# A two-block transformer kernel on one Trainium2 core: rows of the activations' buffer 516 columns apart, and two buffers in the other order

## The chip, the core and the metric

The kernel runs on one core of a Trainium2 chip (trn2) as one launch. The metric is the device time of an execution in microseconds; several runs are made and their median is taken. PE is TensorE, DVE is VectorE, ACT is ScalarE, POOL is GpSimd, SP the engine that issues most DMAs. SBUF is the on-chip memory of 128 partitions; an address in it is a byte offset that is the same in every partition.

## The reference

256 tokens of 1024 features go through two blocks, each of two layers. The first block has a convolution layer and an attention layer, each followed by an MLP; the second has a gated mixer layer and a windowed attention layer with a context of 256 further tokens. Cut to the products of weights and activations, which take nearly all of the work:

```python
def first_block(x, ...):
    for i in range(2):
        h = rms_norm(x, mix_norm_g[i]) * (1.0 + sc1) + sh1
        y = conformer_conv(h, ...) if i == 0 else moba_attention(h, ...)   # 1024 -> 2048, -> 1024; 1024 -> 3072, -> 1024
        x = x + g1 * y
        h = rms_norm(x, mlp_norm_g[i]) * (1.0 + sc2) + sh2
        x = x + g2 * (jnp.square(jax.nn.relu(h @ mlp_w1[i])) @ mlp_w2[i])  # 1024 -> 4096 -> 1024
    return x

def second_block(x, ...):
    for i in range(2):
        h, hc = x * (1.0 + scale) + shift, ctx * (1.0 + scale_c) + shift_c
        out = mixer_a(h, ...) if i == 0 else mixer_b(h, hc, ...)           # 1024 -> 6144, 2048 -> 1024; 1024 -> 2560, -> 1024
        x = layer_norm_2(alpha * x + gate * out, ln_g[i], ln_b[i])
    return x
```

All values are float32. `sh1`, `sc1` and the like are modulation vectors, products of a conditioning vector with a weight matrix.

## The kernel before

The weights are cut into units of 1024 × 256 (`UNITS`), which stream from HBM into four places of `raw` in the order of their use. Activations are kept with features on partitions: a tensor of 1024 features and 256 tokens is 8 tiles (index `k`) of 128 partitions × 256 columns.

A product is made in split precision. An fp32 operand is written as `hi + lo`, both of type float32r, and three products are summed in PSUM: `hi·hi`, `hi·lo`, `lo·hi`. ScalarE writes `w_hi` (L641) and VectorE `w_lo` (L1083) for each unit of weights, two units ahead. The split activations lie in two buffers:

- `X_both`, shape [128, 2, 8, 512]: the input of most units. Index 1 is hi or lo (`XH`, `XL`), index 2 the tile `k`, and of a row's 512 columns the first 256 are the tokens, the others the context's tokens in the second block. One more use: at one place the split weights of a unit are put into columns 256 to 511.
- `F_both`, shape [128, 2, 4096]: the inner activations of the MLPs and of the mixer, and at three places split weights (`AHEAD`). Within a half the rows follow each other at 256 or 512 columns.

PE runs a unit in one of two forms. `three` makes three matmuls for each tile `k` and each half `i` of the unit's columns. `joined`, used by the units of the list `JOINED`, makes two: the first reads hi and lo of the activations as one moving operand of 2 pieces × 256 columns, one half of the buffer's whole length apart.

```python
def three(out, lhs_hi, lhs_lo, rhs_hi, rhs_lo, start, stop):
    mm(out, lhs_hi, rhs_hi, start=start, stop=False)                          # L1894
    mm(out, lhs_hi, rhs_lo, start=False, stop=False)                          # L1895
    return mm(out, lhs_lo, rhs_hi, start=False, stop=stop)                    # L1896
...
def joined(out, lhs_hi, lhs_lo, rhs, start, stop):
    mm(out.rearrange("p (h t) -> p h t", h=2), lhs_hi, rhs, ...)              # L1900, rhs = both[:, :, k, 0:T]
    return mm(out[:, 0:T], lhs_lo, rhs[:, 0, :], ...)                         # L1901
```

For the units that make values (`v`, `b_v`, `a_v`) the activations are the stationary operand, in slices of 128 tokens, and the weights move. Between the products stand boundaries, where a norm is taken and ScalarE and VectorE fill `X_both` tile by tile (`biased_hi` L671, `scale_and_split` L1320 and their like), attention, and the convolution (L1879: plain float32 matmuls, four at a time, over shifted copies of a buffer; a step's start is 4 columns behind the last's).

Buffers are allocated one behind the other in the order in which `sb(...)` names them, and instructions stand in each engine's queue in the order of the code, with semaphores between engines. Before the change `X_both` begins at byte 83072 of a partition and `F_both` at 115840, then follow `V` at 148608, `HT`, `cond`, `dot`, `EV`, `WS`, `BS`, `SM` and the small ones.

Of the kernel before, what the change touches and what calls it, by code (L numbers as in the profile page):

```python
# [28 lines left out]
P = 128  # L29
D = 1024  # L30
KT = D // P
T = 256
# [21 lines left out]
F32R = mybir.dt.float32r  # L54
# [223 lines left out]
def build(nc, stream, first_in, cols_in, cond_in, const_in, x_in, ctx_in, ws_in, bs_in, out):  # L278
    with ExitStack() as ctx:
        def sb(name, shape, dt=F32):  # L280
            return ctx.enter_context(nc.sbuf_tensor(name, shape, dt))
# [6 lines left out]
        w_lo = sb("w_lo", [P, SPLITS, KT, UC], F32R)  # L288
        X = sb("X", [P, KT, T])
        C = sb("C", [P, KT, T])  # L290
        X_both = sb("X_both", [P, 2, KT, 2 * T], F32R)
        F_both = sb("F_both", [P, 2, 2 * KT * T], F32R)
        V = sb("V", [P, 8192])
        HT = sb("HT", [P, KT * T])
        cond = sb("cond", [P, 2, D])
# [63 lines left out]

        U = V[:, 0:KT * (T + PAD)].rearrange("p (k t) -> p k t", k=KT)  # L360
        CV = V[:, 2304:2304 + 2048].rearrange("p (k t) -> p k t", k=KT)
        TS = V[:, 4352:4352 + 2048].rearrange("p (k t) -> p k t", k=KT)

        Q = V[:, 0:2048].rearrange("p (k t) -> p k t", k=KT)
        K1 = V[:, 2048:4096].rearrange("p (k t) -> p k t", k=KT)
        V1 = V[:, 4096:6144].rearrange("p (t c) -> p t c", t=2)

# [2027 lines left out]
```

How the kernel before makes its waits and increments, by code:

```python
        @block.sync  # L577
# [4 lines left out]
            sp.dma_start(col[:, 0:early_cols], cols_in[:, 0:early_cols]).then_inc(params_loaded, 16)  # L582
            sp.dma_start(X[:, :, :], x_in).then_inc(x_loaded, 16)
            for i in range(len(FIRST_CHUNKS)):
                for n in (2 * i, 2 * i + 1):
                    sp.dma_start(first_at[n], first_in[n]).then_inc(first_loaded[n], 16)
                if i in (1, 3, 5):
                    n = i // 2
                    sp.dma_start(raw[:, n, :], stream[n]).then_inc(slot_loaded[n], 16)
            sp.dma_start(col[:, early_cols:], cols_in[:, early_cols:]).then_inc(late_loaded, 16)
            sp.dma_start(con[:, early_con:], const_in[:, early_con:RESIDENT]).then_inc(late_loaded, 16)
            sp.wait_ge(first_dotted, 1)
            for n in range(FIRST_UNITS, NS):
                if EARLY <= n < EARLY + 2:
                    sp.wait_ge(first_dotted, n)
                elif EARLY + 2 <= n < EARLY + 2 + FIRST_UNITS:
                    sp.wait_ge(unit_done, n - EARLY - 1)
                elif n == EARLY + 2 + FIRST_UNITS:
                    sp.wait_ge(unit_consumed, consumed(FIRST_UNITS))
                elif n > EARLY + 2 + FIRST_UNITS:
                    sp.wait_ge(unit_consumed, consumed(n - RING))
                sp.dma_start(places[PLACE[n]], stream[n]).then_inc(slot_loaded[PLACE[n]], 16)
                if n == WHERE[MLP0 + 20]:
                    sp.wait_ge(acts_lo, SET[2])
```

## Time and profile before

| | |
|---|---|
| median of 3 runs | 1204.58 us (1203.28, 1204.62, 1204.58) |
| span of the profiled execution | 1199.6 us; its own time is not listed apart from the three, and 5.0 us lie between the median and the span |
| PE busy | 1173.5 us, 98%, 7486 matmuls |
| DVE, ACT, POOL busy | 910.5 us (76%), 598.2 us (50%), 58.9 us (5%) |
| DMA | 229.48 MB, 191 GB/s over the span |

A matmul's busy time runs from its start until its last result is written, so neighbours overlap, and the pace of PE is to be read from the starts in the timeline. A group of the profile gives line, engine, operation, output and inputs by buffer, the count, and the mean time of one; `X_both,w_hi` as inputs means that both were read, the moving one named first where the shapes say nothing else.

### The profile page before, as it was taken

The page shows a single profiled execution, that of the slowest core. Times are in us where ns is not written, and L with a number is a line of the kernel's source. Part 1 is how long each engine was busy: PE and PEld are TensorE (multiplying, and loading weights), DVE is VectorE, ACT ScalarE, POOL GpSimd, SP SyncE. Part 2 cuts the span into 40 slices and gives each one's busy share as a digit, 9 for nine tenths or more (in the row PEclk, how much of TensorE's full clock was granted, in tenths as well). Part 3 has the DMA queues.
Part 4 walks back from the last instruction along what each step waited for, and adds up shares of the span by engine and source line. Part 5 has one row for each costly group of instructions (what it writes and reads, how often), then busy time and mean ns, then how long its engine had stood idle before and what let it go on. Part 6 is the DMA issues. An engine that isn't in the chain of part 4 may idle for free.

```text
span 1199.6 us, 18278 instructions
## 1 busy us (share of the span) xinstructions
PE 1173.5 (98%) x7486; PEld 1006.4 (84%) x7486; DVE 910.5 (76%) x1372; ACT 598.2 (50%) x800; POOL 58.9 (5%) x85
## 2 busy tenths in 40 slices
PE   8998999999999999999999999999999999999997
PEld 6876988888988868899999888888888888898776
DVE  6798788888888677999977664885856676677757
ACT  4597666546544365865465333232212333454873
POOL 0110000000000040000000000000000000000640
PEclk9999999999999999999999999999999999999998
DMA  9994578787768604777765353342444342343000
GB/s 371 333 340 173 211 282 293 281 313 278 278 241 307 225 21 161 266 261 253 275 238 181 141 194 122 140 150 97 152 164 141 110 155 93 125 141 106 2 1 36
DMA packets 34470, 229.48 MB, mean 191 GB/s; under 512 B 4033, under 2 KB 4801, under 8 KB 8146
## 3 DMA queue, kind: packets, MB, share of 16 engines
q1 hardware_dynamic: 33874, 227.14, 52.1%
q0 software_dynamic: 512, 1.16, 0.4%
q8 instruction: 59, 0.97, 0.3%
q14 instruction: 25, 0.20, 0.0%
HBM read 226.08 MB, written 1.05 MB: 189 GB/s over the span
## 4 chain that ended last, share of the span: by engine, by line
PE 83%; DVE 7%; ACT 5%; issue 2%; DMA 2%; SPq 1%; POOL 1%; ACTq 0%; DVEq 0%
PE prod L1900 17%; PE prod L1894 16%; PE prod L1895 15%; PE prod L1896 15%; PE prod L1901 9%; ACT w_hi L641 2%; DMA WS<-first_chunks 2%; DVE w_lo L1083 1%; PE misc L2056 1%; PE misc L2158 1%; PE misc L1809 1%; PE prod L2146 1%; PE misc L1853 1%; PE prod L2133 1%; DVE raw L1116 1%
## 5 line engine op out<-in xcount | busy, mean ns | idle before, releaser
L1083 DVE TENSOR_TENSOR w_lo<-raw,w_hi 128x2048 fp32r<-128x2048 f32 x129 | 295.4, 2290 | 196.4 <-ACT w_hi L641 196.1
L641 ACT ACTIVATE w_hi<-raw 128x2048 fp32r<-128x2048 f32 x129 | 247.1, 1915 | 379.0 <-PE prod L1896 229.0
L1894 PE MATMUL prod<-X_both,w_hi 128*128 128x256 f32 (+1 forms) x656 | 217.7, 332 | 1.6 <-DVE X_both L1320 1.3
L1895 PE MATMUL prod<-X_both,w_hi 128*128 128x256 f32 (+1 forms) x656 | 214.4, 327 | 0.0
L1896 PE MATMUL prod<-X_both,w_lo 128*128 128x256 f32 (+1 forms) x656 | 214.4, 327 | 0.0
L1900 PE MATMUL prod<-X_both,w_hi 128*128 128x512 f32 x592 | 211.3, 401 | 1.8 <-DVE X_both L1320 1.8
L1901 PE MATMUL prod<-X_both,w_lo 128*128 128x256 f32 x592 | 165.8, 280 | 0.0
L1900 PEld LDWEIGHTS prod<-X_both,w_hi 128*128 128x128 f32 x592 | 111.1, 188 | 32.1 <-DVE X_both L1320 3.0
L1894 PEld LDWEIGHTS prod<-X_both,w_hi 128*128 128x128 f32 x656 | 124.5, 190 | 15.6 <-DVE X_both L1320 1.9
L1895 PEld LDWEIGHTS prod<-X_both,w_hi 128*128 128x128 f32 x656 | 124.5, 190 | 10.8 <-issue 0.5
L1896 PEld LDWEIGHTS prod<-X_both,w_lo 128*128 128x128 f32 x656 | 124.5, 190 | 10.7
L1894 PE MATMUL prod<-F_both,w_hi 128*128 128x256 f32 (+1 forms) x384 | 122.8, 320 | 0.2 <-DVE w_lo L1083 0.2
L1896 PE MATMUL prod<-F_both,w_lo 128*128 128x256 f32 (+1 forms) x384 | 122.3, 318 | 0.0
L1895 PE MATMUL prod<-F_both,w_hi 128*128 128x256 f32 (+1 forms) x384 | 122.3, 318 | 0.0
L1901 PEld LDWEIGHTS prod<-X_both,w_lo 128*128 128x128 f32 x592 | 111.7, 189 | 0.0
L1116 DVE CUSTOM_DVE_ANT_0 raw<-raw,cond 128x1024 f32<-128x1024 f32 x80 | 94.0, 1216 | 0.0
L1900 PE MATMUL prod<-F_both,w_hi 128*128 128x512 f32 x256 | 90.5, 398 | 0.0
L1894 PEld LDWEIGHTS prod<-F_both,w_hi 128*128 128x128 f32 x384 | 72.9, 190 | 5.8 <-DVE w_lo L1083 0.6
L1896 PEld LDWEIGHTS prod<-F_both,w_lo 128*128 128x128 f32 x384 | 72.9, 190 | 5.0
L1895 PEld LDWEIGHTS prod<-F_both,w_hi 128*128 128x128 f32 x384 | 72.9, 190 | 4.9
L1901 PE MATMUL prod<-F_both,w_lo 128*128 128x256 f32 x256 | 71.9, 281 | 0.0
L1894 PE MATMUL prod<-w_hi,X_both 128*128 128x256 f32 (+1 forms) x192 | 66.0, 344 | 0.0
(331 smaller groups left out, 1959.5 us busy)
## 6 DMA issues: line engine op xcount, KB each, us to landing
raw<-stream SPq DMA_DIRECT2D x200, 1024.0 KB, 4.9
V<-first_chunks SPq DMA_DIRECT2D x8, 512.0 KB, 12.0
V<-stream SPq DMA_DIRECT2D x2, 1024.0 KB, 17.4
X<-x_features SPq DMA_DIRECT2D x1, 1024.0 KB, 5.2
raw<-first_chunks SPq DMA_DIRECT2D x2, 512.0 KB, 6.4
C<-first_chunks SPq DMA_DIRECT2D x2, 512.0 KB, 17.1
V<-cond_rows SPq DMA_DIRECT2D x1, 1024.0 KB
C<-ctx_features SPq DMA_DIRECT2D x1, 1024.0 KB, 7.1
```

The lines of the kernel that those rows point to most:

```text
L641: A(halves(w)[0], places[PLACE[n]].rearrange("p (k c) -> p k c", k=KT), ACT.Copy).then_inc(weight_hi, 1)
L1083: ins = tt(lo, places[PLACE[n]].rearrange("p (k c) -> p k c", k=KT), hi.bitcast(F32), ALU.subtract)
L1116: ins = vec.tensor_tensor_reduce(w, w, cond[:, 0, :], 1.0, 0.0, ALU.mult, ALU.add, got[:, 0, k:k + 1])
L1809: ins = mm(misc[:, bank, c:c + T], ones, src[:, k, :], start=(k == 0), stop=(k == count - 1), skip_group_check=True)
L1853: ins = mm(misc[:, b, 0:1], H[:, k, P * b:P * (b + 1)], ones[:, 0:1], start=(k == 0), stop=(k == KT - 1), skip_group_check=True)
L1894: mm(out, lhs_hi, rhs_hi, start=start, stop=False)
L1895: mm(out, lhs_hi, rhs_lo, start=False, stop=False)
L1896: return mm(out, lhs_lo, rhs_hi, start=False, stop=stop)
L1900: mm(out.rearrange("p (h t) -> p h t", h=2), lhs_hi, rhs, start=start, stop=stop)
L1901: return mm(out[:, 0:T], lhs_lo, rhs[:, 0, :], start=False, stop=stop, skip_group_check=True)
L2056: ins = mm(misc[:, i, P * t:P * (t + 1)], VA[:, t, c:c + P], WS[:, j, :], start=True, stop=True)
L2133: ins = mm(score_pair(p)[:, 512 * off:512 * (off + 1)], q, key, start=(term == 0), stop=(term == 2))
```

## The change

The two allocations are written in the other order, and a row of `X_both` becomes 516 columns, of which the last 4 are never used. The code that indexes the buffers is the same, and so are the instructions and their order on every engine.

```diff
@@ build
         X = sb("X", [P, KT, T])
         C = sb("C", [P, KT, T])
-        X_both = sb("X_both", [P, 2, KT, 2 * T], F32R)
         F_both = sb("F_both", [P, 2, 2 * KT * T], F32R)
+        X_both = sb("X_both", [P, 2, KT, 2 * T + 4], F32R)
         V = sb("V", [P, 8192])
```

| bytes in a partition | before | after |
|---|---|---|
| start of `F_both` | 115840 | 83072 |
| start of `X_both` | 83072 | 115840 |
| from a row `k` of `X_both` to the next | 2048 | 2064 |
| from hi to lo in `X_both` | 16384 | 16512 |
| from hi to lo in `F_both` | 16384 | 16384 |
| start of `V` (all behind it moves alike) | 148608 | 148864 |

## Rows read from the trace of the kernel before

**Rows 1.** The page: busy us, share of the span, instructions; PE's granted clock by slices.

```profile
PE 1173.5 (98%) x7486; PEld 1006.4 (84%) x7486; DVE 910.5 (76%) x1372; ACT 598.2 (50%) x800; POOL 58.9 (5%) x85
...
PEclk9999999999999999999999999999999999999998
```

**Rows 2.** The page: the chain that ended last, by engine and by line.

```profile
PE 83%; DVE 7%; ACT 5%; issue 2%; DMA 2%; SPq 1%; POOL 1%; ACTq 0%; DVEq 0%
PE prod L1900 17%; PE prod L1894 16%; PE prod L1895 15%; PE prod L1896 15%; PE prod L1901 9%; ACT w_hi L641 2%; DMA WS<-first_chunks 2%; DVE w_lo L1083 1%; PE misc L2056 1%; PE misc L2158 1%; PE misc L1809 1%; PE prod L2146 1%; PE misc L1853 1%; PE prod L2133 1%; DVE raw L1116 1%
```

**Rows 3.** Lines L1894 and L1900, reads of X_both: count, ns min/median/max, first and last start.

```profile
L1894 PE MATMUL prod<-X_both,w_hi x656: 278/283/681, 45.0 to 1187.6; 128*128 128x256 f32 x96, 128*128 128x512 f32 x68
L1894 PE MATMUL prod<-w_hi,X_both x192: 277/389/792, 388.3 to 1112.4; 128*128 128x256 f32 x96, 128*128 128x512 f32 x96
L1894 PE MATMUL misc<-w_hi,X_both x32: 389/389/389, 685.1 to 744.3; 128*128 128x512 f32 x32
L1894 PE MATMUL prod<-X_both x16: 280/283/467, 1039.3 to 1044.9; 128*128 128x256 f32 x16
...
L1900 PE MATMUL prod<-X_both,w_hi x592: 391/398/504, 145.3 to 1178.7; 128*128 128x512 f32 x198
L1900 PE MATMUL prod<-X_both,F_both x48: 392/395/403, 151.5 to 484.9; 128*128 128x512 f32 x48
```

**Rows 4.** Timeline of PE from 250 us: start us, us, engine line op.

```profile
249.72 0.40 PE L1900 MATMUL prod<-F_both,w_hi 128*128 128x512 f32 x1
249.96 0.28 PE L1901 MATMUL prod<-F_both,w_lo 128*128 128x256 f32 x1
...
250.78 0.40 PE L1900 MATMUL prod<-F_both,w_hi 128*128 128x512 f32 x1
```

**Rows 5.** Timeline of PE from 600 us.

```profile
599.89 0.39 PE L1900 MATMUL prod<-X_both,w_hi 128*128 128x512 f32 x1
600.12 0.28 PE L1901 MATMUL prod<-X_both,w_lo 128*128 128x256 f32 x1
...
600.93 0.39 PE L1900 MATMUL prod<-X_both,w_hi 128*128 128x512 f32 x1
```

**Rows 6.** Stretches, line L1900 alone: us, PE busy (x), PEld, PEclk, DMA, GB/s.

```profile
151.50:298.40 146.90, 146.90 (x417) 78.07 (x417) 1.00 0.80 291
479.75:507.40 27.65, 27.65 (x81) 14.85 (x80) 1.00 0.72 267
...
598.50:609.60 11.10, 11.10 (x32) 5.86 (x32) 1.00 0.72 247
```

**Rows 7.** Timeline of PE from 639.8 us and from 800 us.

```profile
639.73 0.28 PE L1895 MATMUL prod<-F_both,w_hi 128*128 128x256 f32 x1
...
641.17 0.28 PE L1895 MATMUL prod<-F_both,w_hi 128*128 128x256 f32 x1
...
800.25 0.39 PE L1894 MATMUL prod<-X_both,w_hi 128*128 128x512 f32 x1
...
801.38 0.39 PE L1896 MATMUL prod<-X_both,w_lo 128*128 128x512 f32 x1
```

**Rows 8.** Timeline of PE at 90 us; lines L2146, L1609, L1360 and L1305 as rows 3.

```profile
89.78 0.39 PE L1879 MATMUL prod<-V,HT 128*32 128x256 f32 x3
...
91.08 0.39 PE L1879 MATMUL prod<-V,HT 128*32 128x256 f32 x3
...
L2146 PE MATMUL prod<-con,C x64: 272/273/331, 1114.1 to 1159.4; 128*128 128x128 f32 x64
...
L1609 DVE TENSOR_SCALAR C<-C,sm x16: 485/488/490, 1111.5 to 1156.4; 128x512 f32<-128x512 f32 x16
...
L1360 DVE SCALAR_TENSOR_TENSOR V<-prod,col,EV x8: 474/476/485, 44.0 to 86.3; 128x256 f32<-128x256 f32 x8
...
L1305 DVE SCALAR_TENSOR_TENSOR HT<-X,mod,misc x24: 471/474/482, 143.6 to 477.3; 128x256 f32<-128x256 f32 x24
```

## Prediction

> **What bounds the kernel now.** I read the busy shares first. TensorE (PE) is busy 1173.5 us of a span of 1199.6 us, 98%, VectorE 76%, and PE's granted clock stands at its upper level in 39 of the 40 slices [rows 1]. The chain of work that ended last gives the same answer: 83% of it is PE, and its five largest entries are the five lines that multiply split operands, L1894 to L1896 (`three`) and L1900, L1901 (`joined`), 17 + 16 + 15 + 15 + 9 = 72% of the span [rows 2]. So time is made of how far apart these matmuls start. Everything that the change could do to VectorE, ScalarE or a DMA has 26 us of PE idleness as its only way in.
>
> The busy time of a matmul in the groups is its whole passage (398 ns for 512 columns) and overlaps the next; the distance from start to start is what counts, and the timeline has it. Four rhythms matter:
>
> - `joined` pairs (512 columns in two pieces, 256 of `hi` and 256 of `lo`, then 256 columns): in one stretch three pairs take 250.78 − 249.72 = 1.06 us, 353.3 ns a pair [rows 4]. In another three pairs take 600.93 − 599.89 = 1.04 us, 346.7 ns [rows 5]. Both repeat to the nanosecond over whole units; I call them the slow and the quick rhythm. From 151.5 to 298.4 us 416 pairs run (417 less the one cut at the edge) in 146.9 us, 353.1 ns each; from 479.8 to 507.4 us 80 pairs in 27.65 us and from 598.5 to 609.6 us 32 pairs in 11.1 us, 345.6 and 346.9 ns each [rows 6]. I went through all 56 blocks of 16 pairs in the timeline, of which these stretches hold 33: 42 are slow, 11 quick, and 3 are among waits.
> - `three`, 256 columns: 12 starts from 639.73 to 641.17 us, 120.0 ns each. `three`, 512 columns in one piece: 5 starts from 800.25 to 801.38 us, 226 ns each [rows 7].
>
> A quick pair costs what its parts cost, 120 + 226 = 346 ns. A slow one costs 353.3 − 346.7 = 6.7 ns more.
>
> **The change, part by part.** Nothing is removed, added or moved on any engine: every queue holds the same instructions in the same order with the same waits. Only addresses differ. `X_both` rows go from 512 to 516 columns, 2048 to 2064 bytes; its `hi` and `lo` halves from 16384 to 16512 bytes apart; `F_both` takes the old place of `X_both` with its shape unchanged; what is allocated behind (`V`, `HT`, `cond`, `EV`, `WS` and the rest) lies 256 bytes further on. The terms:
>
> 1. *PE reads `X_both` as the moving operand*: 3 × (656 + 16) + 2 × (592 + 48) = 3296 matmuls; *as the stationary operand*: 3 × (192 + 32) = 672 [rows 3]. Together 3968, half of them on an odd k, where a row now starts 16 bytes off any larger power of two. Does the place of a row matter to PE? The trace has three tests. First, the slow rhythm repeats every 3 pairs while k repeats every 8 and the column half every 16: the row's number has no part in it. Second, `F_both` (rows of 1024 bytes) and `X_both` (rows of 2048) show the same 353.3 and 346.7 ns. Third, where operands do start off large powers of two: the convolution reads its shifted rows from a start that moves by 16 bytes with each step of four matmuls, and six such steps take 91.08 − 89.78 = 1.30 us, 216.7 ns each, equal all along; the transposes of the scores read rows 513 columns apart (2052 bytes) and take 272 to 273 ns at the median and minimum in both buffers [rows 8]. These are plain fp32 matmuls, which stream at half the columns per time of the fp32r ones, so the test isn't complete. Taken at 0; bounds below.
> 2. *ScalarE and VectorE write and read `X_both`* in rows of 256 columns at each boundary. Starts off large powers of two leave VectorE as it is: scaling a row of the 513-column buffer takes 485 to 490 ns for starts at 0, 4 and 8 bytes alike; the write into `V` behind 31 columns of padding takes 474 to 485 ns, the write at an even start 471 to 482 ns [rows 8]. At most 5 ns × the 8 tiles of a boundary × 9 boundaries = 0.4 us. Taken at 0.
> 3. *The buffers behind, 256 bytes further on*: their starts keep every divisor up to 256. No row tests more; taken at 0.
> 4. *`F_both` and `X_both` trade places*: both already stood at two different places and gave one rhythm. 0.
>
> Sum: 0 us on a span of 1199.6 us. Around the span lie 1204.58 − 1199.6 = 5.0 us of the median run (the three runs lie from 1.3 below to 0.04 above it). The profiled execution's own time isn't given apart from these, so the sum stands against 1199.6 + 5.0. I take 1204.3 us: the two rhythms can change from one execution to the next, there are 42 slow blocks against 11 quick ones, so a reshuffle has more room downward. One block is worth 16 × 6.7 = 107 ns.
>
> The bounds. Downward: the two-piece read is the only thing that differs between a pair and its parts, and its pieces lie 16384 bytes apart. If that distance makes the 6.7 ns, the slow blocks on `X_both` (28 of the 42, `F_both` having 14) turn quick: 28 × 0.107 = 3.0 us. If the new timing also tips the other 14, 42 × 0.107 = 4.5 us. Upward: if each read or load on an odd k costs one such step of 6.7 ns, 3968 / 2 × 6.7 = 13.3 us.
>
> Further down than that: a `three` matmul of 256 columns takes 120.0 ns, while a column at 2.4 GHz is 0.417 ns and 256 of them 106.7 ns; 13.3 ns go to something. All fp32r operands now start at equal distances from multiples of 512 bytes, so a collision that depends on bits below that couldn't be told from a fixed cost. If it were one and odd k escaped it, 1984 × 13.3 = 26 us would go. I give this 1 in 50: the 512 columns of a `three` (213.3 ns at 2.4 GHz) take 226 ns, so the excess is 13 ns there too, though loads and moving reads lie at other distances in time.
>
> On collisions the Trainium skill ("SBUF — State Buffer", section "SBUF: two separate sides") says that only the port pair of VectorE and GpSimd and the DMA side have contention, and that PE and ACT never wait on anyone. By it the padding can gain nothing and the time stays 1204.6 us; the trace agrees for the DMAs, since the slow pair keeps its 353.1 ns over 146.9 us in which they move 291 GB/s [rows 6]. The same page ("Door 1: The DMA port swizzle") speaks of lines of 16 bytes in SBUF with a penalty for each crossing. 2064 is 129 × 16, so by it a row crosses as many lines as before and the slower rival below falls away; no run here shows it for fp32r.
>
> **The rivals.**
>
> *A, nothing but noise* (forecast): 1204.3 us, its own range 1202.3 to 1206.0. It covers a reshuffle of the rhythms: all 11 quick blocks to slow is +1.2 us, a dozen slow ones to quick −1.3 us, about the spread of the three runs. 0.66.
>
> *B, the pieces 16384 bytes apart collide*: 1201.6 us if `X_both` alone heals, 1200.1 us if all does. For it: the excess sits in the two-piece matmul alone. From its start to the next matmul's it takes 249.96 − 249.72 = 0.24 us in the slow rhythm [rows 4] and 600.12 − 599.89 = 0.23 us in the quick one [rows 5]. Against it: the same 16384 bytes give 346.7 ns elsewhere, on both buffers, so the distance doesn't decide by itself; how a block is entered does. 0.16, with the 26 us case 0.02 more.
>
> *C, the other side: odd rows cost PE a step.* The mechanism is one extra fetch at the start of a row that lies 16 bytes off, in the L1894 to L1901 matmuls. Full price +13.3 us, 1217.9 us; if only the 640 two-piece reads pay, on odd k and at both pieces, 320 × 2 × 6.7 = 4.3 us, 1208.9 us. It decides (over 0.2%, 2.4 us) from 360 steps of 6.7 ns on. Against it the evenness of the convolution and of the 513-column rows. 0.12, and 0.04 for a slower shift that I can't name.
>
> **How the numbers follow.** A measurement of this kernel can tell about 0.2%, 2.4 us, from no change: below 1202.2 is faster, above 1207.0 slower. A gives 0.66 same. B's cases both lie below 1202.2: with the 26 us case 0.18 faster. C and the unnamed shift 0.16 slower. The range takes in A and both ends of B, down to 1199.8, and upward A and the edge of the same: 1207.0. Left out are C and the 26 us case.
>
> **What the changed kernel's profile would show.** If A: `joined` pairs at 353.3 or 346.7 ns and nothing between, 120 and 226 ns for `three`, on odd and even k alike; PE busy within 1 us of 1173.5 us plus or minus the count of slow blocks times 0.107 us. If B: 346.7 ns in all pairs on `X_both`, and still 353.3 ns in some on `F_both`. If C: a start-to-start distance that alternates with k on `X_both` and not on `F_both`. The groups of ScalarE and VectorE on `X_both` keep their means within 5 ns in each case. I'd be wrong if row starts below 512 bytes matter to fp32r reads at full rate, which no row of before can show.

## The result and the profile after

The changed kernel takes 1206.87 us (median of 20 runs, 1203.75 to 1209.19); the kernel before takes 1204.2 us in 20 runs (1202.31 to 1208.32). The ratio is 1.0017 with a 95% interval of 1.0010 to 1.0025: 1.2 to 3.0 us slower (2.0 by the ratio; the two medians differ by 2.7), small and real.

The page of the changed kernel, its busy times and the chain by line:

```profile
span 1204.2 us, 18278 instructions
...
PE 1179.6 (98%) x7486; PEld 1006.3 (84%) x7486; DVE 910.7 (76%) x1372; ACT 598.4 (50%) x800; POOL 58.9 (5%) x85
...
PE prod L1900 17%; PE prod L1894 15%; PE prod L1895 15%; PE prod L1896 15%; PE prod L1901 8%; ACT w_hi L641 2%; DMA WS<-first_chunks 2%; DVE w_lo L1083 1%; PE misc L2056 1%; PE misc L1809 1%; PE misc L2158 1%; PE prod L2146 1%; PE prod L2133 1%; DVE raw L1116 1%; PE prod L1861 1%
```

VectorE and ScalarE stand where they stood [rows 1]; PE is busy 6.1 us longer, but busy time doesn't tell the effect: two kernels below whose paces are those of before (`h1_order_look`, `i1_all_32`) had 1177.8 and 1178.5 us. This execution took 1205.98 us, 1.8 us more than its span, so the profiled one of before, with its 1199.6 us, took an estimated 1201.4 us, less than any of the 20 listed, and the two profiles exaggerate the difference.

The timeline of PE in the changed kernel, at both ends of five stretches of 24 matmuls within one unit (start us, us, engine, line):

```profile
180.87 0.40 PE L1900 MATMUL prod<-X_both,w_hi 128*128 128x512 f32 x1
...
185.05 0.39 PE L1900 MATMUL prod<-X_both,w_hi 128*128 128x512 f32 x1
...
622.04 0.28 PE L1894 MATMUL prod<-F_both,w_hi 128*128 128x256 f32 x1
...
624.92 0.28 PE L1894 MATMUL prod<-F_both,w_hi 128*128 128x256 f32 x1
...
704.28 0.40 PE L1894 MATMUL prod<-w_hi,X_both 128*128 128x512 f32 x1
...
709.88 0.40 PE L1894 MATMUL prod<-w_hi,X_both 128*128 128x512 f32 x1
...
912.57 0.39 PE L1894 MATMUL prod<-X_both,w_hi 128*128 128x512 f32 x1
...
918.14 0.39 PE L1894 MATMUL prod<-X_both,w_hi 128*128 128x512 f32 x1
...
1060.60 0.28 PE L1894 MATMUL prod<-X_both,w_hi 128*128 128x256 f32 x1
...
1063.42 0.28 PE L1894 MATMUL prod<-X_both,w_hi 128*128 128x256 f32 x1
```

Divide each stretch by its 24 matmuls. 512 columns moving from `X_both`: 5.57 us, 232 ns each, where rows 7 have 226. 512 columns of weights against a stationary slice of `X_both` (`w_hi,X_both`): 5.60 us, 233 ns. 256 columns from `X_both`: 2.82 us, 117.5 ns, where 120.0 stood on either buffer. 256 columns from `F_both`: 2.88 us, 120.0 ns as before [rows 7]. Pairs on `X_both`: 4.18 us for 12, 348.3 ns, neither of the rhythms of [rows 4, 5]. All that touches the padded buffer has a new pace, in both directions, and on `F_both` the `three` matmuls keep the old ones.

Means over all matmuls of a kind (from the starts in the timeline, those behind a wait left out), in ns:

| start to start | count | before | after | count × difference |
|---|---|---|---|---|
| 512 columns moving from `X_both` | 816 | 226.8 | 231.5 | +3.8 us |
| 512 columns of weights, `X_both` stationary | 384 | 226.8 | 232.7 | +2.3 us |
| 256 columns moving from `X_both` | 1152 | 119.8 | 117.6 | −2.6 us |
| 256 columns of weights, `X_both` stationary | 288 | 119.8 | 118.3 | −0.4 us |
| pairs on `X_both` (592 and 48) | 640 | 351.8 | 349.1 | −1.7 us |
| pairs on `F_both` | 256 | 352.6 | 349.2 | −0.9 us |
| 256 and 512 columns on `F_both` | 1152 | 120.0, 226.8 | 120.0, 226.9 | 0 |

They add up to +0.5 us, short of the measured 2.0. The two rows of pairs depend on how many of the 56 blocks happened to be slow in the one execution of before that was profiled: 44 with the 3 blocks among waits sorted in. Two experiments below with the same distances between operands had 28 and 41. With 28 instead of 44, before would be 1.7 us shorter in those rows, and the sum +2.2 us; with 41 it would be +0.8 us.

The two spans differ by more, 4.5 us. Matmul by matmul, the starts give +0.7 us in the steady stretches of the five lines, +0.9 us in the waits among them and +2.9 us in the matmuls outside of them. Much of the last two is PE's granted clock (the figure ahead of the last two; the first two lines are of before, the others of after):

```profile
325.00:335.00 10.00, 9.18 (x68) 8.36 (x68) 5.15 (x12) 2.95 (x9) 0.00 (x0) 1.00 0.56 211
465.00:475.00 10.00, 9.53 (x69) 8.46 (x67) 5.74 (x15) 3.62 (x10) 0.00 (x0) 1.00 0.56 211
...
325.00:335.00 10.00, 9.78 (x60) 8.70 (x58) 4.12 (x13) 3.01 (x8) 0.00 (x0) 0.83 0.55 211
465.00:475.00 10.00, 10.00 (x61) 8.99 (x60) 5.52 (x16) 4.09 (x10) 0.00 (x0) 0.83 0.57 210
```

The levels of the clock are 1.2 and 2.4 GHz, so 0.83 over 10 us is the lower one for an estimated third of the time. Ahead of the last 15 us, the execution before had such a fall in one place (near 110 us), the one after in four (near 100, 140, 330 and 470 us). From 135 to 152 us the changed kernel loses 1.5 us and from 300 to 345 us 1.0 us. The falls don't go with the padding: `h1_order_look` and `i1_all_32`, with the paces of before, had them in five and four places, and `f2_rows_only`, with the paces of after, in two. It keeps 1.00 from 325 to 335 us and loses nothing from 300 to 345 us.

ScalarE and VectorE write the padded rows at the old pace, to within 1 and 4 ns at the median (lines L671 and L1320 of the changed kernel; count, ns min/median/max):

```profile
L671 ACT ACTIVATE X_both<-HT,mod x24: 491/509/514, 144.9 to 477.0; 128x256 fp32r<-128x256 f32 x24
...
L1320 DVE SCALAR_TENSOR_TENSOR X_both<-HT,mod,X_both x24: 476/480/486, 145.5 to 477.5; 128x256 fp32r<-128x256 f32 x24
```

### The profile page after: what moved, and what is told of

It is laid out like the page before. It is cut to its first block, busy times and chain, and to the rows that moved or that the text cites. A ratio compares the mean times of both kernels' runs of the same rounds, so it can differ in the third digit from the quotient of the medians.

```text
span 1204.2 us, 18278 instructions
## 1 busy us (share of the span) xinstructions
PE 1179.6 (98%) x7486; PEld 1006.3 (84%) x7486; DVE 910.7 (76%) x1372; ACT 598.4 (50%) x800; POOL 58.9 (5%) x85
## 4 chain that ended last, share of the span: by engine, by line
PE 81%; DVE 8%; ACT 5%; issue 2%; DMA 2%; SPq 1%; POOL 1%; ACTq 0%; DVEq 0%
PE prod L1900 17%; PE prod L1894 15%; PE prod L1895 15%; PE prod L1896 15%; PE prod L1901 8%; ACT w_hi L641 2%; DMA WS<-first_chunks 2%; DVE w_lo L1083 1%; PE misc L2056 1%; PE misc L1809 1%; PE misc L2158 1%; PE prod L2146 1%; PE prod L2133 1%; DVE raw L1116 1%; PE prod L1861 1%
## 5 line engine op out<-in xcount | busy, mean ns | idle before, releaser
L1894 PE MATMUL prod<-X_both,w_hi 128*128 128x256 f32 (+1 forms) x656 | 217.8, 332 | 2.3 <-DVE X_both L1320 1.3
L1900 PE MATMUL prod<-X_both,w_hi 128*128 128x512 f32 x592 | 209.5, 397 | 0.2 <-DVE X_both L1320 0.2
L1894 PEld LDWEIGHTS prod<-X_both,w_hi 128*128 128x128 f32 x656 | 123.2, 188 | 18.3 <-DVE X_both L1320 1.9
L1900 PEld LDWEIGHTS prod<-X_both,w_hi 128*128 128x128 f32 x592 | 111.2, 188 | 28.5 <-DVE X_both L1320 0.8
L1894 PE MATMUL prod<-F_both,w_hi 128*128 128x256 f32 (+1 forms) x384 | 122.8, 320 | 0.2 <-DVE w_lo L1083 0.2
L1900 PE MATMUL prod<-F_both,w_hi 128*128 128x512 f32 x256 | 89.8, 396 | 0.0
L1894 PEld LDWEIGHTS prod<-F_both,w_hi 128*128 128x128 f32 x384 | 73.1, 190 | 6.0 <-DVE w_lo L1083 0.8
L1894 PE MATMUL prod<-w_hi,X_both 128*128 128x256 f32 (+1 forms) x192 | 66.4, 346 | 0.0
```

The lines of the kernel that those rows point to most:

```text
L1900: mm(out.rearrange("p (h t) -> p h t", h=2), lhs_hi, rhs, start=start, stop=stop)
```

## The experiments

"Distance" below is the start of the moving operand minus that of the stationary one, modulo 256 bytes. In the kernel before it is 0 for all large matmuls: `w_hi`, `w_lo`, `X_both` and `F_both` begin at 33920, 50304, 83072 and 115840, all 128 past a multiple of 256, and their rows and slices are multiples of 512 or 256 bytes long. Line numbers shift by 1 or 2 where the edit adds lines.

### The parts of the change, one at a time

**The order alone** (`f1_order_only`, `h1_order_look`)

```diff
-        X_both = sb("X_both", [P, 2, KT, 2 * T], F32R)
         F_both = sb("F_both", [P, 2, 2 * KT * T], F32R)
+        X_both = sb("X_both", [P, 2, KT, 2 * T], F32R)
```

> The two buffers in the other order, rows still 512 columns apart. Theory T1 (what counts is where a row of X_both starts within a small power of two): every start is again a multiple of 128 bytes, so the distances from start to start go back to those of before, 120.0 and 226.8 ns for three, and 346.7 or 353.3 ns for a joined pair; time within 1.2 us of before. Rival T2 (the place of the buffers or the 256 bytes by which the rest moves counts): 231.5 ns for 512 columns on X_both and +2 us as in the changed kernel. Rival T3 (only the share of slow and quick joined rhythms moved, by chance): 226.8 ns too, time anywhere within 2 us.

> The order alone again, for its profile (that of the run before was of a disturbed execution at half pace throughout; its other times were level with the kernel before). T1: 120.0 and 226.8 ns for three on both buffers, joined pairs at 346.7 or 353.3 ns. T2: 231.5 ns for 512 columns on X_both.

Ratio 1.0004 (0.9994 to 1.0014). `h1_order_look` is one more execution of the same kernel, 1203.31 us beside 1203.5, and its timeline shows:

```profile
910.49 0.39 PE L1894 MATMUL prod<-X_both,w_hi 128*128 128x512 f32 x1
...
915.93 0.39 PE L1894 MATMUL prod<-X_both,w_hi 128*128 128x512 f32 x1
```

24 matmuls in 5.44 us, 226.7 ns. Over all of them 226.8 and 119.8 ns, and 28 slow blocks, 26 quick. T2 falls: the order costs nothing. T1 holds, and T3 (chance alone) isn't told from it here.

**The rows alone** (`f2_rows_only`)

```diff
-        X_both = sb("X_both", [P, 2, KT, 2 * T], F32R)
+        X_both = sb("X_both", [P, 2, KT, 2 * T + 4], F32R)
         F_both = sb("F_both", [P, 2, 2 * KT * T], F32R)
```

> Rows 516 columns apart, the buffers in the old order (F_both and all behind it then start 256 bytes further on). T1: the changed kernel's distances on X_both return, near 231.5 ns for 512 columns, 117.6 ns for 256, 232.7 ns for 512 columns of weights against a stationary slice of X_both; F_both stays at 120.0 and 226.8 ns; +2 us (1 to 3). T2 (place or order): as before the change, 226.8 and 120.0 ns. T3: 226.8 and 120.0 ns, time within 2 us.

Ratio 1.0013 (1.0002 to 1.0024).

```profile
912.61 0.39 PE L1894 MATMUL prod<-X_both,w_hi 128*128 128x512 f32 x1
...
918.18 0.39 PE L1894 MATMUL prod<-X_both,w_hi 128*128 128x512 f32 x1
```

5.57 us, and over all: 231.5, 232.7 (weights moving) and 117.6 ns, the paces of the changed kernel to a tenth. `F_both`, which lies 256 bytes further on here, keeps 119.9 and 226.9 ns: a shift by 256 bytes is none. T1 holds so far; T2 and T3 fall.

### How far a start has to be off

**A constant shift** (`f3_base_16`)

```diff
+        gap_a = sb("gap_a", [P, 4])
         X_both = sb("X_both", [P, 2, KT, 2 * T], F32R)
+        gap_b = sb("gap_b", [P, 60])
         F_both = sb("F_both", [P, 2, 2 * KT * T], F32R)
```

> The old order and rows of 512 columns, but X_both starts 16 bytes further on (and 240 bytes are left behind it, so F_both and the rest move by 256). All rows then lie 16 bytes off a multiple of 64, alike for each k. T1 in the form 'a start off the boundary costs': 512 columns on X_both over 230 ns at every k with no alternation, +6 us or more than the changed kernel has from its 512-column matmuls, since there a quarter of the rows are on the boundary. T1 in the form 'what costs is that the offset changes from row to row': 226.8 and 120.0 ns at a constant offset, time as before. T5 (what counts is the offset between X_both and the weights read beside it): a new constant distance, either side of 226.8 ns.

The allocator rounds starts up to 32 bytes, so this kernel has both activation buffers at a distance of 32 bytes from the weights, alike for each k; it isn't the kernel that its expectation speaks of. Ratio 1.0026 (1.0016 to 1.0036).

```profile
911.67 0.40 PE L1896 MATMUL prod<-X_both,w_hi 128*128 128x512 f32 x1
...
917.27 0.40 PE L1896 MATMUL prod<-X_both,w_hi 128*128 128x512 f32 x1
...
1062.54 0.28 PE L1896 MATMUL prod<-X_both,w_hi 128*128 128x256 f32 x1
...
1065.34 0.28 PE L1896 MATMUL prod<-X_both,w_hi 128*128 128x256 f32 x1
```

512 columns: 5.60 us for 24, 233.3 ns, 6.6 more than at distance 0. 256 columns: 2.80 us, 116.7 ns, 3.3 less. All joined blocks are quick, 346.7 ns, but for the three whose weights lie in `F_both` and so moved along (distance 0, 353.3 ns). A steady offset has its own steady pace: what matters is not that the offset changes from row to row. It is what T5 said. Against the profiled execution before, the 512-column matmuls lose 10.3 us and all others win 10.0, so their paces alone give +0.3 us (+1.8 against `h1_order_look`); the measured 3.1 us (1.9 to 4.3) is more, and the rest isn't accounted for.

**Rows of 520 and of 528 columns** (`f4_rows_520`, `h4_rows_528`): the changed kernel with `2 * T + 8` and `2 * T + 16`; in the second `bst` lies in `GX` for room.

> As the changed kernel with rows of 520 columns: starts at 0 and 32 bytes within 64, by turns of two. T1 with a boundary of 64 bytes: distances off 226.8 and 120.0 ns again, repeating every 2 tiles k. T1 with a boundary of 32 bytes: all rows on it, 226.8 and 120.0 ns, time as before. T2 and T3 as in the run with the order alone.

> The changed kernel with rows of 528 columns (2112 bytes), so that each row starts on a multiple of 64 again; the small buffer bst lies in GX to make room. With a boundary of 64 bytes: 120.0 and 226.8 ns, joined pairs at 346.7 or 353.3 ns, time of before within 1.2 us. With a boundary of 128 bytes: 512 columns at 230 to 233 ns, repeating every 2 tiles k, +2 to +4 us.

Ratios 1.0032 (1.0019 to 1.0046) and 1.0026 (1.0017 to 1.0036). With 520 columns the 512-column matmuls on `X_both` take 232.4 ns, those of 256 columns 118.3 ns. With 528, where each row starts on a multiple of 64 and every second one 64 off a multiple of 128:

```profile
913.75 0.39 PE L1894 MATMUL prod<-X_both,w_hi 128*128 128x512 f32 x1
...
919.31 0.39 PE L1894 MATMUL prod<-X_both,w_hi 128*128 128x512 f32 x1
```

5.56 us, 231.7 ns. Boundaries of 32 and of 64 bytes both fall; being on a multiple of 64 isn't enough.

**16 bytes, by slicing** (`h2_start_16`)

```diff
-        X_both = sb("X_both", [P, 2, KT, 2 * T], F32R)
+        X_room = sb("X_both", [P, 2 * KT * 2 * T + 16], F32R)
...
+        X_both = X_room[:, 4:4 + 2 * KT * 2 * T].rearrange("p (h k t) -> p h k t", h=2, k=KT)
```

> Rows of X_both 512 columns apart, all of them shifted by 16 bytes by slicing from a larger buffer; F_both stays on multiples of 64. (In the run called f3_base_16 the allocator rounded each start up to 32 bytes, so there X_both, F_both and all behind them lay 32 bytes off a multiple of 64; it gave 233.3 ns for 512 columns and 116.7 to 117.3 ns for 256 on both buffers, and quick joined pairs throughout.) T6, what counts is the distance modulo 64 bytes between the moving operand's start and the stationary one's: a constant distance between 226.8 and 233.3 ns for 512 columns on X_both and between 116.7 and 120.0 for 256, with F_both at 120.0 and 226.8. T7, only 32 bytes count and 16 do not: 226.8 and 120.0 ns.

Ratio 1.0013 (0.9999 to 1.0026).

```profile
619.75 0.28 PE L1895 MATMUL prod<-F_both,w_hi 128*128 128x256 f32 x1
...
622.47 0.28 PE L1895 MATMUL prod<-F_both,w_hi 128*128 128x256 f32 x1
...
909.22 0.39 PE L1895 MATMUL prod<-X_both,w_hi 128*128 128x512 f32 x1
...
914.78 0.39 PE L1895 MATMUL prod<-X_both,w_hi 128*128 128x512 f32 x1
```

`X_both`: 231.7 ns for 512 columns, 113.3, 116.7 or 118.7 for 256 by unit, 346.7 or 360.0 a pair. T7 falls; T6 had the 512 columns right, but 113.3 ns lies below its 116.7. `F_both` didn't stay where it was, as I had meant: the 64 bytes of slack put it at distance 64, and there 24 matmuls of 256 columns take 2.72 us, 113.3 ns (117.8 in other units), 512 columns 228.9, and the pairs 353.3.

### Which operand's start counts

**The weights moved instead** (`h3_weights_32`): room between the two slots of `w_hi` and `w_lo`, and

```diff
+            c = (UNIT + 16) * (w % SPLITS) + (0 if UNITS[w][0] in WIDE else 8)
-            return w_hi[:, w % SPLITS], w_lo[:, w % SPLITS]
+            return [m[:, c:c + UNIT].rearrange("p (k c) -> p k c", k=KT) for m in (w_hi, w_lo)]
```

> Activations as before; the split weights of each unit whose matmuls move 256 columns or joined pairs start 32 bytes off a multiple of 64, those of units that move 512 columns stay on it. T6 (the distance between the two operands' starts counts): 256 columns at 117 ns instead of 119.8 (2208 matmuls, 6 us), joined pairs at 346.7 ns throughout (some 850 pairs at 5 ns, 4.5 us), 512 columns unchanged at 226.8; about 10 us faster, 1194 us. T8 (the moving operand's own start counts, the stationary one's doesn't): 119.8 ns and both joined rhythms, no change but for the value units, whose weights move: 1204 us.

Ratio 1.0048 (1.0035 to 1.0061), the slowest of all and far from my 1194. I had the sign of the distance wrong (moving minus stationary is −32 here, not +32), the second slots lay another 64 bytes off, and `w_lo` had moved by 128. The last makes one clean reading: a wide unit in the first slot has `w_hi` at distance 0 and `w_lo` at 128, the activations where they were.

```profile
913.26 0.39 PE L1896 MATMUL prod<-X_both,w_hi 128*128 128x512 f32 x1
...
918.81 0.39 PE L1896 MATMUL prod<-X_both,w_hi 128*128 128x512 f32 x1
```

5.55 us, 231.3 ns instead of 226.7. So the stationary operand's start counts (T8 falls), and 128 bytes count where 256 did not.

**Everything by 32 bytes** (`i1_all_32`): `in_front = sb("in_front", [P, 8])` ahead of `raw`.

> A spare tensor of 8 columns in front of everything: the weights, X_both, F_both and all the rest start 32 bytes further on, with all distances between them as before. T6 (only the distance between the moving and the stationary operand's start counts, modulo 256 bytes): 120.0 and 226.8 ns, joined pairs at 346.7 or 353.3, time of before within 1.2 us. T9 (each operand's own start within 256 bytes counts too): 512 columns above 230 ns or 256 columns below 118 ns, and the time off by 2 us or more to either side.

```profile
910.60 0.39 PE L1895 MATMUL prod<-X_both,w_hi 128*128 128x512 f32 x1
...
916.04 0.39 PE L1895 MATMUL prod<-X_both,w_hi 128*128 128x512 f32 x1
...
1057.49 0.28 PE L1895 MATMUL prod<-X_both,w_hi 128*128 128x256 f32 x1
...
1060.37 0.28 PE L1895 MATMUL prod<-X_both,w_hi 128*128 128x256 f32 x1
```

226.7 and 120.0 ns, 41 slow blocks and 13 quick, ratio 0.9992 (0.9978 to 1.0005). For a shift by 32 bytes it is the distance between the operands that counts and not where each lies. T9 falls for this shift.

**Distance +32 made by the weights** (`i2_weights_back_32`), and **+16 for some** (`i3_weights_back_16`): as `h3_weights_32` with slots 2112 columns apart, so that both arrays keep their place modulo 256, and 56 (or 60) for the 8.

> Activations as before; the split weights of the units that move 256 columns or joined pairs start 224 bytes past a multiple of 256 from where they did, so the moving operand's start minus the stationary one's is +32 modulo 256, as in the run f3_base_16; weights of units that move 512 columns keep distance 0 (bst lies in GX to make room). T6: 256 columns at 116.7 ns, joined pairs at 346.7 ns, 512 columns at 226.8; three-256 saves some 6 us, joined 4.5 us, so about 1194 us. T9: other distances, 256 columns anywhere from 113 to 119 ns and pairs up to 351 ns as in h3_weights_32.

> As i2_weights_back_32, but 240 bytes (moving minus stationary +16) for the units that make three matmuls of 256 columns, and 224 for joined pairs. T6: 113.3 or 116.7 ns for 256 columns, as X_both had in h2_start_16, 346.7 ns for a pair, 226.8 for 512; 1190 to 1193 us. T9: nothing can be said beforehand beyond 113 to 119 ns.

```profile
179.91 0.39 PE L1902 MATMUL prod<-X_both,w_hi 128*128 128x512 f32 x1
...
184.06 0.39 PE L1902 MATMUL prod<-X_both,w_hi 128*128 128x512 f32 x1
...
617.67 0.28 PE L1896 MATMUL prod<-F_both,w_hi 128*128 128x256 f32 x1
...
620.47 0.28 PE L1896 MATMUL prod<-F_both,w_hi 128*128 128x256 f32 x1
```

The same unit on `F_both` in `i3_weights_back_16`:

```profile
621.46 0.28 PE L1896 MATMUL prod<-F_both,w_hi 128*128 128x256 f32 x1
...
624.34 0.28 PE L1896 MATMUL prod<-F_both,w_hi 128*128 128x256 f32 x1
```

In `i2_weights_back_32` 12 pairs take 4.15 us, 346 ns each, and 256 columns 116.7 ns, as forecast; 512 columns stay at 226.8. 1195.48 us, ratio 0.9926 (0.9908 to 0.9945). The second missed: 256 columns at "distance 16" take 120.0 ns (2.88 us for 24), some 117.3, not the 113.3 to 118.7 that `X_both` showed when it was the one to move; 1198.08 us, ratio 0.9941 (0.9922 to 0.9961). At 16 bytes the distance alone doesn't give the pace, so T6 fails as a general rule and holds for the distances of 0 and +32 that were made in two ways.

### A version that beats both

**Activations of narrow units 32 bytes further right** (`i4_views_32`). Rows stay 512 columns apart and no buffer in front of `F_both` moves. The parts that only 256-column and joined matmuls read are written and read 8 columns further on; operands of 512 columns keep distance 0.

```diff
+        XHn, XLn = X_both[:, 0, :, 8:], X_both[:, 1, :, 8:]
-        F_hi = FH[:, :].rearrange("p (b k t) -> p b k t", b=2, k=KT)
+        F_hi = F_both[:, 0, 8:8 + 2 * KT * T].rearrange("p (b k t) -> p b k t", b=2, k=KT)
...
                         hi, lo, both = XH, XL, X_both
+                        if w < MIX_A or w >= B_OUT:
+                            hi, lo, both = XHn, XLn, X_both[:, :, :, 8:]
```

> Rows of 512 columns and all buffers where they were; the activations of units that move 256 columns (all of the first block and the last unit set) are put 8 columns further right in their rows of X_both, those of the MLPs 8 columns further in F_both (whose halves are 64 columns longer), while the operands of 512 columns keep their place. Both T6 and T9 say what f3_base_16 showed for these operands: 256 columns at 116.7 ns, joined pairs at 346.7, and 226.8 for 512 columns; 33 units of 48 matmuls at 3 ns less, 56 blocks of pairs at 5.5 ns less a pair: 9 us off, 1195 us. If only chance moved the rhythms: 1204 us.

```profile
179.98 0.39 PE L1901 MATMUL prod<-X_both,w_hi 128*128 128x512 f32 x1
...
184.14 0.39 PE L1901 MATMUL prod<-X_both,w_hi 128*128 128x512 f32 x1
...
618.62 0.28 PE L1895 MATMUL prod<-F_both,w_hi 128*128 128x256 f32 x1
...
621.42 0.28 PE L1895 MATMUL prod<-F_both,w_hi 128*128 128x256 f32 x1
...
903.63 0.39 PE L1895 MATMUL prod<-X_both,w_hi 128*128 128x512 f32 x1
...
909.07 0.39 PE L1895 MATMUL prod<-X_both,w_hi 128*128 128x512 f32 x1
```

346.7 ns a pair and no slow block, 116.7 and 226.7 ns. 1195.46 us, ratio 0.9927 (0.9907 to 0.9947): 8.8 us faster than before where 9 were forecast. In the profiled executions the starts of the large matmuls, waits included, add up to 955.6 us before and 948.1 us here, 7.5 less; their steady stretches alone give 9.6 less.

## Why the prediction went wrong, point by point

- **The number and the mechanism.** The 1206.87 us lie just inside the stated 1199.8 to 1207.0, but that is no credit to the forecast. It said 1204.3 us and no effect on PE; there is one, in the direction that was given 0.16, and it is small only because a loss and a gain nearly cancel.
- **What bounds the kernel** was right. The change acted through PE's pace and through nothing else that the profiles show.
- **Term 1, PE's reads of `X_both`, taken at 0**, is the step that failed. "Does the place of a row matter to PE?" was answered with three tests, and none of them held what it was asked to. The first and the second compared rows that all lie at distance 0 modulo 256 (1024, 2048 and 16384 are multiples of it), which can't tell anything of other distances. The third had other distances but plain fp32 matmuls. Those columns pass at about half the rate (216 ns from start to start for 256 plain fp32 columns, against 120.0), and evenness there said nothing of fp32r. I named this gap and still gave the zero. In place of 0 the trace shows +6.1 us on 512-column matmuls and −4.7 us on the rest of `X_both`, part of the −1.7 us of the pairs in it being chance; the whole came to 2.0 us.
- **Rival C** had the kind of thing right (row starts cost PE) and the form wrong. It isn't a step paid on odd rows at any width: 512 columns pay 4.7 to 5.9 ns on average, 256 columns gain 1.5 to 2.3. Its sign was a distance that alternates with `k`. What the trace has is one that changes with `k` in no such order: by tile and by matmul within the tile, 512 columns moving from `X_both` take 225.2 to 235.2 ns and 256 columns 113.6 to 121.4, and `f2_rows_only` repeats each of these means within 0.5 ns (units whose eight tiles follow each other). Hence neither +13.3 nor +4.3 us came out but about +2.
- **Rival B** blamed the 16384 bytes between the pieces. They don't make the excess by themselves: with 16384 bytes between the halves, `f3_base_16` has all pairs at distance +32 at 346.7 ns, and its three slow blocks are those at distance 0. At distance 0 both rhythms occur (44, 28 and 41 slow blocks of 56 in one execution each of three kernels with it). In `i2_weights_back_32` 2 were slow, both at distance 0, in `i4_views_32` none. The excess isn't bound to distance 0 either: in `h2_start_16` the 16 blocks on `F_both`, at 64, were slow, and some on `X_both`, at 16, took 360.0 ns. The reading for this rival, that the excess sits in the two-piece matmul alone (0.24 against 0.23 us), rests on two rounded rows. Over all slow and quick blocks of before, 5.5 ns lie there (236.6 against 231.1 ns) and 1.2 in the other (116.8 against 115.6), so a quick pair is also not 226 + 120 in its parts.
- **The 13.3 ns beyond 256 columns at 2.4 GHz**, to which I gave 1 in 50 of being a matter of low bits: part of it is. At steady other distances 116.7 and 113.3 ns were measured, so 3.3 to 6.7 of the 13.3 can be had, but the padding had most of its rows in 512-column use, where it costs.
- **Terms 2 to 4** were right. ScalarE's groups on `X_both` kept their medians within 1 ns and VectorE's within 4 (484 against 480 ns in the one furthest off), the order alone gave a ratio of 1.0004, and a move by 256 bytes changed no pace.
- **What lies around the span** was mis-sized: 1.8 us and not 5.0; the profiled execution was itself faster than the three runs shown. The sign set for "no effect", PE busy within 1 us of 1173.5, couldn't have served: it was 1177.8 us in `h1_order_look`, with the paces of before.
- **What the Trainium skill says** ("SBUF — State Buffer", "SBUF: two separate sides"), that PE and ACT never wait on anyone, would have given 1204.6 us; the measured shift is small but outside it. Its lines of 16 bytes ("Door 1: The DMA port swizzle") don't decide here either: rows 516, 520 and 528 columns apart start on multiples of 16, 32 and 64 bytes and all pace differently from rows 512 apart.

Left open: why the distance acts as it does. The weight load and the moving read run at the same time, and the distance between their starts bears on the pace, which fits a collision of two address streams; no run shows the collision itself. Distances of 48, 96 and 128 bytes occur by turns in the changed kernel, but none was held steady for both operand kinds, and why 16 bytes give different paces by which operand moved isn't known.

Nor do the paces of one profiled execution give every time. For nine kernels their sum, against before, lies within 2.1 us of the measured difference. For three the measured time is longer than their paces say: `f3_base_16` (+0.3 by the paces, +3.1 measured), `h3_weights_32` (+2.7, +5.8) and `h2_start_16` (−2.4, +1.6). How much of that is waits, the clock or a different rhythm in the other executions no run shows.

## What to carry to other kernels

Where PE bounds a kernel, measure the distance from start to start of its matmuls and not their durations: a few nanoseconds on each of thousands is the time. Treat the start of the moving operand relative to the stationary one, modulo 256 bytes, as a thing to tune per width of matmul; here +32 bytes won for 256 columns and for pairs, and 0 for 512. Before two profiled executions are compared by their spans, look at how often the granted clock fell in each. Before a term is set to zero because "rows at different places show the same pace", check that the places differ in the bits that the change touches.

## What the runs showed of the hardware

- Steady fp32r matmuls with a new stationary operand each time: 226.7 ns for 512 columns at distance 0 and 233.3 at +32 bytes; 120.0 ns for 256 columns at 0, 116.7 at +32 bytes, 113.3 in some units at 16 and 64. At −32 bytes (`f3_base_16`, weights moving) 512 columns take 233.3 and 256 columns 118.3. At mixed distances the means lie between (231.5, 117.6).
- Most steady paces are multiples of 6.67 ns, or of half of it: 113.3, 116.7, 120.0, 226.7, 233.3, 346.7, 353.3, 360.0. 6.67 ns are 16 cycles at 2.4 GHz, and the granted clock was 1.00 throughout these stretches.
- At one distance a pair of matmuls can run in either of two rhythms for tens of units, 6.7 ns or 107 ns a block apart, without a wait in sight. Three kernels with the same distances had 44, 28 and 41 slow blocks of 56 in one execution each, worth up to 1.7 us. That the way into a stretch decides is likely but not shown.
- The granted clock falls in some places of one execution and not of another of like kernels, mostly near a boundary: 0.83 against 1.00 from 325 to 335 us. The stretches around two such falls were 1.0 and 1.5 us longer than in the execution without them.
